# Norm factors turned into rows by two small DMAs through DRAM instead of by TensorE

## The reference, cut to what matters

```python
def rms_norm(x, g):
    xf = x.astype(jnp.float32)
    y = xf * lax.rsqrt(jnp.mean(xf * xf, axis=-1, keepdims=True) + RMS_EPS)
    return (y * g.astype(jnp.float32)).astype(x.dtype)

def swiglu(x, w_gate, w_up, w_down):
    return (jax.nn.silu(x @ w_gate) * (x @ w_up)) @ w_down

for layer in range(DEPTH):          # the first four blocks
    h = rms_norm(x, norm_mix_pre[layer])
    h = neighbourhood_attention(h, ...) if layer % 2 == 0 else dilated_attention(h, ...)
    x = x + rms_norm(h, norm_mix_post[layer])
    h = rms_norm(x, norm_ffn_pre[layer])
    x = x + rms_norm(swiglu(h, ...), norm_ffn_post[layer])
```

## Time and profile before

| what | value |
|---|---|
| median of three runs | 1744.44 us |
| span of the profiled execution | 1743.1 us (the page gives no other time of it) |
| TensorE busy | 1736.3 us, 10086 matmuls |
| VectorE busy | 1230.6 us |
| ScalarE busy | 988.6 us |
| GpSimd busy | 110.1 us |
| moved by DMA | 314.74 MB, mean 181 GB/s |
| chain that ended last | TensorE 99% |

### The profile page before, as it was taken

The page is one execution under the profiler, slowest core; times in us unless marked ns, Lnnn a source line. Parts: engine busy times, 40 slices in busy tenths (PEclk is TensorE's granted clock), DMA queues, the critical chain, the costliest instruction groups (busy, mean ns, idle before and its releaser), DMA issues.

```text
span 1743.1 us, 25490 instructions
## 1 busy us (share of the span) xinstructions
PE 1736.3 (100%) x10086; PEld 1495.9 (86%) x10086; DVE 1230.6 (71%) x1901; ACT 988.6 (57%) x1585; POOL 110.1 (6%) x191
## 2 busy tenths in 40 slices
PE   9999999999999999999999999999999999999999
PEld 7888888888888888888888888888888888888887
DVE  5877765668886777467756887775587648878762
ACT  6666554645555655365545666554565447666551
POOL 1100000702210000000001010000000001100000
PEclk9999999999999999999999999999999999999999
DMA  9445554544343555545554345555355534335552
GB/s 328 181 159 213 188 220 164 223 184 155 146 158 123 192 193 218 193 157 194 192 195 149 121 145 199 195 188 215 145 206 189 213 137 168 131 145 218 193 218 73
DMA packets 45496, 314.74 MB, mean 181 GB/s; under 512 B 5040, under 2 KB 5552, under 8 KB 8384
## 3 DMA queue, kind: packets, MB, share of 16 engines
q1 hardware_dynamic: 45056, 312.54, 48.1%
q10 hardware_dynamic: 288, 0.52, 0.1%
q0 software_dynamic: 32, 0.03, 0.0%
HBM read 312.03 MB, written 1.05 MB: 180 GB/s over the span
## 4 chain that ended last, share of the span: by engine, by line
PE 99%; DMA 0%; DVE 0%; ACT 0%; issue 0%; SPq 0%
PE P L449 97%; PE P L457 1%; PE P L760 1%; DMA raw<-w_all 0%; PE P L661 0%; PE P L1111 0%; PE P L1191 0%; PE P L466 0%; PE P L1057 0%; PE P L1134 0%; PE P L1005 0%; DVE xs L1896 0%; ACT wh L1293 0%; PE P L995 0%; PE P L1006 0%
## 5 line engine op out<-in xcount | busy, mean ns | idle before, releaser
L1841 DVE TENSOR_TENSOR wl<-raw,wh 128x2048 fp32r<-128x2048 f32 x287 | 656.9, 2295 | 185.0 <-ACT wh L1287 166.1
L1287 ACT ACTIVATE wh<-raw 128x2048 fp32r<-128x2048 f32 x291 | 552.2, 1901 | 195.7 <-PE P L449 172.1
L449 PE MATMUL P<-xx,wh 128*128 128x512 f32 (+2 forms) x2800 | 643.2, 384 | 0.0
L449 PEld LDWEIGHTS P<-xx,wh 128*128 128x128 f32 (+1 forms) x2800 | 505.7, 188 | 96.5
L449 PE MATMUL P<-xx,wl 128*128 128x256 f32 x2688 | 350.7, 284 | 0.0
L449 PEld LDWEIGHTS P<-xx,wl 128*128 128x128 f32 x2688 | 340.3, 191 | 10.4 <-issue 0.3
L1416 ACT ACTIVATE ft<-P 128x256 f32<-128x256 f32 x240 | 90.2, 382 | 229.7 <-PE P L449 229.7
L449 PE MATMUL P<-wh,fhh 128*128 128x512 f32 x528 | 206.3, 391 | 0.0
L449 PE MATMUL P<-wl,fhh 128*128 128x512 f32 x528 | 205.6, 389 | 0.0
L449 PE MATMUL P<-wh,fhl 128*128 128x512 f32 x528 | 205.6, 389 | 0.0
L2004 DVE TENSOR_TENSOR fg<-P,ft 128x256 f32<-128x256 f32 x240 | 101.7, 424 | 121.2 <-ACT ft L1416 117.2
(11 more groups left out here) (333 smaller groups left out, 1469.9 us busy)
## 6 DMA issues: line engine op xcount, KB each, us to landing
raw<-w_all SPq DMA_DIRECT2D x289, 1024.0 KB, 4.8
nB<-rpb SPq DMA_DIRECT2D x4, 512.0 KB, 8.6
raw<-w_all SPq DMA_DIRECT2D x2, 512.0 KB, 6.7
xs<-x_in SPq DMA_DIRECT2D x1, 1024.0 KB, 8.6
fgb<-post SPq DMA_DIRECT2D x2, 512.0 KB, 5.6
out<-xs SPq DMA_DIRECT2D x4, 256.0 KB, 2.0
C<-cst SPq DMA_DIRECT2D x1, 769.5 KB, 7.1
ntm<-x_in ACTq DMA_DIRECT2D x2, 256.0 KB, 5.1
```

The costliest lines, as they stand in the source:

```text
L449: return t_.on.matmul(o, l, r, start=start, stop=stop, skip_group_check=True)
L1287: a.on.activation(o, i, ACT.Copy).then_inc(*hi.up((m,)))
L1841: v.on.tensor_tensor(o, i, h.bitcast(F32), ALU.subtract).then_inc(*lo.up(m))
```

## The change

The transposes of `rr`, the bank that they need and the copy to `rb` are taken out at all ten stages. In their place GpSimd writes `rr` to a row of 256 words in DRAM (`rrow`, one row for each stage), waits for that to land, and reads the row back with 128 copies of it, one for each partition, into `rb`. In stage 2 it also reads the row back twice more, in the dilated order, into the two halves of `rp`, in place of the two tiny matmuls and their copy. The users of `rb` and `rp` wait for the transfers.

```diff
+        s_row, s_rb = signal("s_row", 16), signal("s_rb", 16)
+        s_rp = [signal(f"s_rp{a}", 16) for a in range(2)]
...
+        rrow = nc.dram_tensor("rrow", [10, S], F32, kind="Internal").ap()
...
-            def factors(s, b=6):
-                claim(b)
-                t_.wait_ge(*gx.of("r", s))
-                for t in range(2):
-                    k = t_.on.transpose(P[b][:, toks(t)], rr_[:, t:t + 1].broadcast_to([128, 128]), ident)
-                k.then_inc(*tx.up(("rb", s)))
-                held[b] = [(vx, "rb", s)]
...
-                        if z == 1 and m == 0:
-                            claim(0)
-                            t_.wait_ge(*vx.of("rbp", 2))
-                            for t in range(2):
-                                k = mul(P[0][:, t:t + 1], AD["drb"][0:1, toks(t)], one[0:1, :], True, True)
-                            k.then_inc(*tx.up(("rr", 2)))
-                            held[0] = [(vx, "rr", 2)]
...
-            def factors(s, b=6):
-                v.wait_ge(*tx.of("rb", s))
-                v.on.tensor_copy(rb[:, :], P[b][:, 0:256]).then_inc(*vx.up(("rb", s)))
...
-                    v.wait_ge(*vx.of("rb", s))
+                    v.wait_ge(*s_rb.of(s))
...
-                v.wait_ge(*tx.of("rr", 2))
-                v.on.tensor_copy(rp_[:, :], P[0][:, 0:2]).then_inc(*vx.up(("rr", 2)))
...
-                    v.wait_ge(*vx.of("rr", 2))
+                    for i in range(2):
+                        v.wait_ge(*s_rp[i].of(2))
...
                 root(rr_[:, :], 0, 2, ss[:, 4:6], D, gx, gx.of("sum", s), ("v", s), ("r", s), ax.of("root", s))
+                g.wait_ge(*gx.of("r", s))
+                g.on.dma_start(rrow[s].rearrange("(t p) -> p t", t=2), rr_[:, :], allow_slow_non_contiguous=True).then_inc(*s_row.up(s))
+                g.wait_ge(*s_row.of(s))
+                g.on.dma_start(rb[:, :], rrow[s:s + 1, :].broadcast_to([128, S])).then_inc(*s_rb.up(s))
+                if s == 2:
+                    for a in range(2):
+                        g.on.dma_start(rp_[64 * a:64 * a + 64, :],
+                                       rrow[s].rearrange("(j a t) -> a j t", a=2, t=2)[a]).then_inc(*s_rp[a].up(s))
                 if s in FFNS and s not in POST:
-                    g.wait_ge(*gx.of("r", s))
                     g.on.tensor_scalar(rh_[:, :], rr_[:, :], 0.5, None, ALU.mult).then_inc(*gx.up(("rh", s)))
```

More of the change, by code:

```diff
@@ L573, in first_two @@
                 put(s, m, banks[0], 4, 8)
-                factors(s)
                 put(s, m + 1, banks[1], 4, 8)
@@ L852, in na @@
                     held[2 + i] = [(aa, "V", 0, i)]
-                factors(0)
                 for f in range(8):
@@ L937, in dil @@
                     held[banks[i // 2][i % 2]] = [(aa, "V", 2, 0, i)]
-                factors(2, 3)
                 for z in (1, 2):
@@ L1583, in dil @@
                     if z == 1:
-                        a.wait_ge(*vx.of("rr", 2))
+                        for i in range(2):
+                            a.wait_ge(*s_rp[i].of(2))
                     a.wait_ge(*mm.of("piece", b0 + 4 * z + 3))
@@ L2151, in na @@
                 v.wait_ge(*s_prm.of(0))
-                factors(0)
                 rq = AN["nrb"]
-                v.wait_ge(*vx.of("rb", 0))
+                v.wait_ge(*s_rb.of(0))
                 v.on.tensor_scalar(rq[:, 0, :], rb[:, :], 0.125, None, ALU.mult)
@@ L2203, in dil @@
                 ahead(b0 + 4)
-                factors(2, 3)
                 ahead(b0 + 5)
                 enter(2)
-                v.wait_ge(*vx.of("rb", 2))
+                v.wait_ge(*s_rb.of(2))
                 v.on.tensor_copy(near(AD["drb"][:, :]), far(rb[:, :])).then_inc(*vx.up(("rbp", 2)))
-                v.wait_ge(*tx.of("rr", 2))
-                v.on.tensor_copy(rp_[:, :], P[0][:, 0:2]).then_inc(*vx.up(("rr", 2)))
                 def evict(z, banks):
                     v.wait_ge(*mm.of("piece", b0 + 4 * z + 3))
-                    v.wait_ge(*vx.of("rr", 2))
+                    for i in range(2):
+                        v.wait_ge(*s_rp[i].of(2))
                     for hf in range(2):
@@ L2233, in part @@
                     if z or j == 0:
+                        v.wait_ge(*vx.of("rbp", 2))
                         r = AD["drb"][:, :]
@@ L2664, in pool_program @@
                 means(s + 2)
-        signals = s_raw + [s_first] + s_x[0] + s_x[1] + [s_ident, s_prm, s_cst, s_gu, s_dist] + s_rpb + [s_res, s_post] + s_out[0] + s_out[1]
+        signals = s_raw + [s_first] + s_x[0] + s_x[1] + [s_ident, s_prm, s_cst, s_gu, s_dist, s_row, s_rb] + s_rp + s_rpb + [s_res, s_post] + s_out[0] + s_out[1]
         signals += [mm, tx, ta, th, hi, ax, aa, af, ah, lo, vx, va, vf, vh, gx, ga, gh]
```

## The result

The changed kernel takes 1832.0 us (median of 5, 1828.0 to 1839.1) against 1744.4 (5 runs, 1744.2 to 1744.6). The ratio is 1.0505, 95% interval 1.0494 to 1.0516: 87.6 us slower, where 7.5 were forecast.

The account below looks back on a forecast made before the run. TensorE's instruction list was taken to bound the kernel: -2.8 (removed) + 6.8 (hybrids) + 3.5 (stage 2) = +7.5 us on the 1743.1 span, plus 1.3 to the median, gives 1752. The 8-in-10 range was 1745 to 1762.

Parts of the forecast that it names:

- L: Every stage: time from GpSimd having the factors in `rr` until their row stands in `rb`; taken as 5.9 us.
- 2 x (2.2 + 0.73) = 5.9: Write and read of the row: each a 2.2 us transfer of the read's shape plus 0.73 us of GpSimd's issue.
- upper bound of 12.0: Row's delay at most 2 x 6.0 us, from the only transfer GpSimd issued, at the start among the first weights.
- L - 2.46: Hybrid stages 5 and 8: TensorE's wait before turning `hex`, 3.4 us each, 6.8 for both, bounds 2.3 to 19.
- has no price here: Whole kernel: a longer stop may lower TensorE's clock; no slice of the trace showed it, so nothing was counted.
- Nothing is lost until L is about 10: Feed-forward stages 6, 7 and 9: product 1.0 us late, 5.4 us in hand before TensorE's low parts, so no loss.
- Stage 2: Dilated attention: GpSimd's casts start late behind the DMA issues, TensorE waits 3.5 us for the first `dxp`; range 0 to 7.9.
- The other stages: nothing: Stages 1, 3 and 4 use the row some 12.8 us later, stage 0 waits for first weights anyway: no loss.
- rival B: Long transfers: the row's packets queue beside a weight transfer, delay about 9 us, +16 us, 1761; chance 0.19.
- What is removed: TensorE's list: ten transpose pairs of 0.21 us and 0.73 us of row turning in stage 2, 2.8 us saved.
- A: Rival, short transfers: delay about 4.0 us, hybrids 3.1 and stage 2 about 0.9, +1.2 us, 1746; chance 0.14.
- C: Rival: the chain over `hex` does not stop TensorE, only the shorter list is left, 1741.6 us; chance 0.05.

Follow-up runs that it names:

- m_readonly: Changed kernel without the ten row writes and their wait; the broadcast reads a constant row written once at the start: 1756.0 us, ratio 1.0064.
- m_far: Changed kernel with each factor written 64 bytes from the next, landing waited for, then a constant row broadcast: 1770.7 us, ratio 1.0149.
- m_sbuf: Changed kernel with the row kept in one partition of on-chip memory instead of DRAM, all ten stages: 1782.2 us, ratio 1.0215.
- m_best6: Kernel before with the row by transfers through on-chip memory in stages 1, 3, 4, 6, 7 and 9 only: 1754.1 us, ratio 1.0054.
- m_late: Kernel before, no added transfer; in stages 5 to 9 the row's users wait for 22 small GpSimd fills: 1788.7 us, ratio 1.0250.
- m_synth: Kernel before plus the crowded row write in all stages and a wait of 23 to 28 fills in all but stage 2, no broadcast: 1818.4 us, ratio 1.0419.
- micro1: Program that computes nothing, timing single transfers alone and beside 1 MB loads: 256 words side by side 9.9 us, 64 bytes apart 2.0.
- m_write: Kernel before, transposes and copy kept, with the change's row write added in all ten stages and read by nobody: 1766.4 us, ratio 1.0124.
- m_best134: Kernel before with the row by transfers through on-chip memory in stages 1, 3 and 4 only: 1744.1 us, ratio 0.9999.

## Why the prediction was wrong

Us from the start of the factors' last instruction to the start of the row's first use, and what the stage lost:

```
            stage 5       stage 8       stages 6, 7, 9
before      2.5 ->  0     2.5 ->  0     5.1 ->  0
m_readonly  5.0 ->  5.0   4.9 ->  3.6   5.1 -> -0.4 -0.4 -0.4
m_far       8.4 ->  8.0   8.4 ->  8.0   8.5, 8.2, 8.5 -> 0.6 0.3 0.5
m_sbuf     12.1 -> 13.2  12.7 -> 12.2  10.1, 10.4, 10.2 -> 3.8 4.0 2.3
m_best6     2.5 -> -0.1   2.5 ->  0    10.4, 10.1, 10.1 -> 2.5 3.6 3.7
m_late     13.6 -> 13.7  13.6 -> 12.6  13.0 -> 6.7 6.7 5.0
m_synth    16.3 -> 15.9  15.2 -> 14.2  16.4, 17.5, 17.5 -> 8.5 10.0 11.7
changed    16.5 -> 17.3  15.0 -> 13.7  16.4, 17.9, 17.7 -> 10.8 9.9 11.7
```

- **The step that failed is the size of L, "2 x (2.2 + 0.73) = 5.9".** It was 16.3 us in stage 5, above even the upper bound of 12.0: 11.0 from the issue of the write to that of the read, and 5.0 to the first use. I took the time of a transfer by its bytes (128 and 68 KB) and said that I had no row for 256 single words; the bound of 6.0 each was a row of another shape and held nothing for them. micro1 has 9.9 for this write alone against 1.5 for the same 1 KB in one piece. The crowd is not all of it: m_far, with a write of 2.5 us, still had L = 8.2, so my 5.9 was too small for an uncrowded pair too.
- **The hybrids' formula, L - 2.46, was right as to the wait.** In the table each us beyond 2.5 costs about one, over m_late's bare lateness as over the transfers; 1.2 to 3.6 us come on top. At the measured L it gives 13.9 and 12.4; TensorE's idle time in the two stages rose by 14.1 and 11.2, and the whole loss was 17.3 and 13.7. The place was partly wrong: TensorE stops first at the low part behind the product (11.2 us), which I had named as queued there, and at `hex` only for the rest.
- **The clock "has no price here" was the part on top.** In stage 5 the granted clock stayed at 0.50 for some 16 us, half of them with TensorE at work, and TensorE's busy time rose by 3.2 us there, by 2.5 in stage 8 and by 20.4 over the kernel, although its list was shorter. It follows from the stop, not from the transfers: m_late has it without one (4.0 us more busy time in stage 5, 2.9 in stage 8).
- **"Nothing is lost until L is about 10" in stages 6, 7 and 9** was right in kind: nothing at 5 us. The table puts the point near 8, not 10 (m_best6 loses 2.5 to 3.7 at 10). Past it each us costs 1.0 to 1.8: 32.5 us in the three, forecast as 0. This slack was spent by L, and no rival had L beyond it.
- **Stage 2: 3.5 forecast, 8.3 measured.** The casts started late as said (at 334.97, 11.3 us after the factors and not 5.1, see below), and TensorE waited 6.6 us for the first `dxp`. But m_write, whose casts are on time, loses 8.2 there through late weights: two causes in one place, and the parts of each in the 8.3 are not separated. The timeline of GpSimd, which answers to the earlier trace rows:

```profile
323.51 0.19 POOL L2535 TENSOR_TENSOR rr<-rr,nw 128x2 f32<-128x2 f32 x1
324.00 0.77 POOL L2544 DMA_DIRECT2D rrow<-rr  x1 [0.29 <-POOL rr L2535]
333.34 0.57 POOL L2546 DMA_DIRECT2D rb<-rrow  x1 [8.57 <-DMA rrow<-rr]
333.90 1.10 POOL L2549 DMA_DIRECT2D rp<-rrow  x2
334.97 9.57 POOL L2567 CAST dxp<-xx 128x256 fp32r<-128x256 f32 x16
```

- **"The other stages: nothing".** Stages 0, 1, 3 and 4 cost 15.8 us. The row was in time, as predicted for 1, 3 and 4 (m_best134: nothing lost), but the crowded write held up the weights: m_write, in which nobody waits for the row, loses 13.3 us in these four. That the change's own traffic could delay the weights was weighed in rival B only the other way round, as weights delaying the row.
- **What is removed** is right: stages with the short list and no lateness are 0.1 to 0.4 us shorter (m_readonly, m_best134), as 0.21 for a pair said.
- **The rivals.** B had the direction, long transfers, at half the size; its reason, packets queued beside the weights, fits the read (3.1 alone, 5.7 beside a stream) but not the write, which takes 9.9 with nothing beside it. A's L of about 4 no version reached: transfers of 1.5 to 2.0 us exist alone, but beside a stream the 1 KB takes 5.0 and the far words 5.3, and the uncrowded pair of m_far has L = 8.2. C never came near.

Together: 31.0 in the hybrids, 32.5 in stages 6, 7 and 9, 8.3 in stage 2, 15.8 in 0, 1, 3 and 4: 87.6, where the forecast had 6.8, 0, 3.5 and 0, less 2.8.

## What to carry to other kernels

Price a transfer by its pieces, where they lie and what runs beside it, not by its bytes: 256 words from 128 partitions side by side in DRAM took 9.9 us alone and, beside a stream of loads, set that back by an estimated 4.8 us; the same words 16 bytes apart took 2.0 alone. If the profile has no row of that shape, a row of another shape is no bound for it. Where TensorE is busy all the time, the rows give the slack of each stage; compare it with the whole range of the delay, not its likely value, and add what the lower clock takes after each stop, here 1 to 4 us.

## What I had not expected of the hardware

- The crowded write: 32, 128, 256 and 512 words take 5.6, 8.4, 9.9 and 9.9 us, on GpSimd's queue and on SyncE's alike (10.0 for 256); into a partition of the on-chip memory 128 take 1.9.
- While it is outstanding, 1 MB transfers of another queue can go at a fraction of their rate: 44 and 33 GB/s in stage 4 where there were 147 and 412, and 234 to 266 beside the stream of micro1 where there were 426.
- Ten added writes of 256 far words or 128 far pairs, read by nobody, cost 1 us in some executions and 8 to 10 in others. The kernel before, timed beside them, stays within 1744.2 and 1745.1.
